# Gate and up matrices loaded as two halves of 64 partitions with 16 KB runs instead of two halves of 128 partitions with 8 KB runs

## The reference, cut to what matters

```python
D_MODEL = 1024; SEQ = 256; DEPTH = 2; N_EXPERTS = 16; D_EXPERT = 512
"moe_w_gate": nrm(ks[21], (DEPTH, N_EXPERTS, D, D_EXPERT), D),
"moe_w_up":   nrm(ks[22], (DEPTH, N_EXPERTS, D, D_EXPERT), D),
"moe_w_down": nrm(ks[23], (DEPTH, N_EXPERTS, D_EXPERT, D), D_EXPERT),

    for e in range(N_EXPERTS):
        hdn = jax.nn.silu(xt @ w_gate[e]) * (xt @ w_up[e])
        y = y + combine[:, e:e + 1] * (hdn @ w_down[e]).astype(jnp.float32)
```

## Time and profile before

| | us |
|---|---|
| time before, median of 3 runs | 886.97 (886.14 to 888.75) |
| the profiled execution | 886.78 |
| its span | 885.0 |
| busy in the span: PE | 842.0 |
| DVE | 329.7 |
| ACT | 177.5 |
| POOL | 159.8 |

### The profile page before, as it was taken

One profiled execution on the slowest core, in us unless ns is written; L12 is line 12 of the kernel. 1 busy time (PEld: TensorE's weight loads), 2 busy tenths in 40 slices (PEclk: granted clock), 3 DMA queues, 4 the chain that ended last, 5 costly groups with the idle time before them and its releaser, 6 DMA issues.

```text
span 885.0 us, 11785 instructions
## 1 busy us (share of the span) xinstructions
PE 842.0 (95%) x4341; PEld 465.4 (53%) x4341; DVE 329.7 (37%) x598; ACT 177.5 (20%) x356; POOL 159.8 (18%) x269
## 2 busy tenths in 40 slices
PE   5999999999999899999999869999899999999996
PEld 3788444444444455455545337774545555545552
DVE  2835766856302322111112058777511112211114
ACT  2100112112102221222121132240322122112112
POOL 0023000000003531122210122300632212012111
PEclk9999999999999999999999899999899999999999
DMA  9989999998569599999999996679889999989994
GB/s 317 387 308 375 375 363 337 339 380 346 230 244 372 206 405 422 421 420 422 422 422 420 371 403 264 238 292 423 324 331 421 422 421 420 384 317 422 421 404 129
DMA packets 70014, 317.29 MB, mean 359 GB/s; under 512 B 10039, under 2 KB 10170, under 8 KB 44366
## 3 DMA queue, kind: packets, MB, share of 16 engines
q1 hardware_dynamic: 61594, 304.42, 85.7%
q0 software_dynamic: 4976, 8.40, 3.1%
q10 hardware_dynamic: 3396, 3.80, 1.4%
HBM read 311.31 MB, written 15.20 MB: 369 GB/s over the span
## 4 chain that ended last, share of the span: by engine, by line
PE 81%; DMA 8%; SPq 5%; DVE 3%; issue 2%; ACT 1%; ACTq 0%; POOL 0%; DVEq 0%; POOLq 0%
PE bank L730 12%; PE bank L912 12%; PE bank L930 11%; PE bank L899 10%; PE bank L771 6%; PE bank L874 6%; PE bank L671 5%; SPq L470 4%; PE bank L1129 3%; DMA acc<-in_moe_w_up 3%; DMA ring<-in_w_mod 2%; PE bank L723 2%; DMA part<-outs 1%; PE bank L1083 1%; PE bank L922 1%
## 5 line engine op out<-in xcount | busy, mean ns | idle before, releaser
L1793 DVE TENSOR_TENSOR arena<-bank,arena 128x256 f32<-128x256 f32 x34 | 21.0, 617 | 254.4 <-PE bank L912 254.4
L1542 DVE SCALAR_TENSOR_TENSOR part<-ring,cpad,part 128x1024 f32<-128x1024 f32 x84 | 111.1, 1323 | 4.1 <-DMA ring<-in_w_mod 1.2
L730 PE MATMUL bank<-ring,xnT 128*128 128x512 f32 x256 | 111.2, 592 | 0.0
L899 PE MATMUL bank<-ring,arena 128*64 128x512 f32 x416 | 92.1, 595 | 0.0
L930 PE MATMUL bank<-ring,arena 128*64 128x512 f32 x352 | 81.7, 606 | 4.3 <-issue 4.3
L912 PE MATMUL bank<-ring,arena 128*64 128x256 f32 x704 | 80.3, 381 | 0.2 <-issue 0.2
L730 PEld LDWEIGHTS bank<-ring,xnT 128*128 128x128 f32 x256 | 48.4, 190 | 59.4 <-issue 59.3
L874 PEld LDWEIGHTS bank<-arena,y 128*128 128x128 f32 x544 | 64.6, 198 | 15.4 <-issue 15.4
L874 PE MATMUL bank<-arena,y 128*128 128x128 f32 x544 | 67.5, 284 | 1.4 <-DVE arena L1753 1.4
L912 PEld LDWEIGHTS bank<-ring,arena 128*64 128x64 f32 x704 | 50.2, 137 | 30.2 <-issue 8.6
L1317 ACT ACTIVATE arena<-bank,modc,scale 128x128 f32<-128x128 f32 x68 | 25.6, 457 | 182.5 <-PE bank L874 182.5
(11 more groups left out here) (342 smaller groups left out, 1066.9 us busy)
## 6 DMA issues: line engine op xcount, KB each, us to landing
ring<-in_w_mod SPq DMA_DIRECT2D x48, 1024.0 KB, 12.3
ring<-in_moe_w_gate SPq DMA_DIRECT2D x48, 1024.0 KB, 15.5
ring<-in_moe_w_down SPq DMA_DIRECT2D x44, 1024.0 KB, 12.7
ring<-in_moe_w_up SPq DMA_DIRECT2D x40, 1024.0 KB, 12.7
ring<-in_ret_w_in SPq DMA_DIRECT2D x24, 1024.0 KB, 7.4
arena<-in_moe_w_down SPq DMA_DIRECT2D x12, 1024.0 KB, 17.0
arena<-in_moe_w_up SPq DMA_DIRECT2D x12, 1024.0 KB, 16.6
arena<-in_moe_w_gate SPq DMA_DIRECT2D x9, 1024.0 KB, 10.5
```

The lines of the kernel that those rows point to most:

```text
L730: ins = pe.matmul(pair[tt][:], xnT[:, k, tok(tt)], w[:, k, :], start=(k == 0), stop=(k == KT - 1))
L899: ins = pe.matmul(bank[0][e * 64:(e + 1) * 64, :], xgT[:, k, e * 64:(e + 1) * 64], w(e, k), start=(k == 0), stop=(k == KT - 1))
L1542: ins = dve.scalar_tensor_tensor(o, w[:, k, :], c, o, ALU.mult, ALU.add)
```

## The change

For a gate or up matrix whose buffer is undivided, a transfer now carries all 16 KB of 64 partitions (0 to 63, then 64 to 127), where it carried 8 KB of all 128. The bytes, the number of transfers and their order are the same. Since each transfer now brings all rows for half of the partitions, a product needs both: `landed_in` waits for both at each call, and SyncE, before it refills a buffer, waits for the event of the second half in both cases when either of the two matrices is loaded in this way. Down matrices, and gate and up matrices in divided buffers, are loaded as before.

```diff
+        def in_one_piece(l, m):
+            return m % 6 < 4 and HOMES[l][m][0] <= RING
...
                 def fill(m, f):
                     w = matrix(l, m // 6, m % 6)
-                    w = w[:, 4 * f:4 * f + 4, :] if m % 6 < 4 else w[:, f]
                     b = HOMES[l][m][0]
-                    sp.dma_start(home(l, m, f), w).then_inc(landed[f][b] if b < RING else outside_in[f][b - RING], 16)
+                    if in_one_piece(l, m):
+                        ps = slice(f * P // 2, (f + 1) * P // 2)
+                        dst = (ring[:, b, :] if b < RING else arena[:, spare:spare + 4096]).rearrange("p (k n) -> p k n", k=KT)[ps]
+                        w = w[ps]
+                    else:
+                        dst = home(l, m, f)
+                        w = w[:, 4 * f:4 * f + 4, :] if m % 6 < 4 else w[:, f]
+                    sp.dma_start(dst, w).then_inc(landed[f][b] if b < RING else outside_in[f][b - RING], 16)
...
-                        used(m - n, f, begun)
+                        used(m - n, 1 if in_one_piece(l, m) or in_one_piece(l, m + 1) else f, begun)
...
                 def landed_in(m, f):
                     b, n = HOMES[l][m]
-                    pe.wait_ge(landed[f][b] if b < RING else outside_in[f][b - RING], 16 * n)
+                    for g in range(2) if in_one_piece(l, m) else (f,):
+                        pe.wait_ge(landed[g][b] if b < RING else outside_in[g][b - RING], 16 * n)
```

## The result

The changed kernel takes 1227.36 us (1218.08 to 1229.53, four runs) where the kernel before took 887.15 beside it: a ratio of 1.382, with a 95% interval of 1.3779 to 1.3861. The prediction was 1070, with a range of 884 to 1100. The direction was right, the size was not: 340 us more, where 183 had been forecast.

A forecast was written before the change was run, and what follows sets the result against it. The DMA queue was taken to bound layer 0's experts and nearly layer 1's. Layer 0 +78 and layer 1 +97 made 175, plus 8 for less lead: +183, so 886.8 becomes 1070 us, range 884 to 1100.

The forecast's parts named there:

- What bounds the kernel: Expert rounds: the DMA queue needs 29.9 us a pair against TensorE's 25.94, setting layer 0's end; layer 1 just favours TensorE.
- The price of a transfer: Each 64-partition transfer of 16 KB runs, bounded from 0.05 us gained to 2.49 us more; 2.25 us more taken.
- the high end of the bounds: Transfers to half the partitions fill half the lanes: 210 GB/s, 4.98 us each, 2.49 more.
- 1.9: Cost factor taken for each new transfer, 2.25 us more, since engines somewhat out of step can fill other lanes part-time.
- Layer 0: Layer 0's experts: 34 loop transfers at 2.25 give 76.5 us, plus 2 for those ahead: +78.
- The idle 28.6 us: Queue idle time between 223 and 305, said to take up the 27 us more of 12 transfers ahead of layer 0's experts.
- Layer 1: Layer 1's experts: 56 transfers cost 126 us more, less idle time and lead: +97; 8 more for less lead on entering and leaving.
- The late refills: Layer 1: SyncE waits for the gate product's end, 3.5 us later, seven times; 0 to 3 us if the queue keeps pace.
- The attention only moves: Attention between the layers: it is only shifted in time, with nothing added.
- an unchanged pace: Rival 1, expert loads: nothing happens to the pace; layer 0 gains 1.7 us, total 885 to 888; chance 0.23.
- the partial case: Rival 2, expert loads: factor 1.6 from long runs, or engines drifting; 1.49 us a transfer, +105, 992; chance 0.13.
- worse than half: Rival 3, expert loads: 4.98 us a transfer plus other queue traffic, 1095, more if halves collide; beyond 1100 chance 0.07.

The follow-up runs named there:

- kept in groups: SyncE waits in the loop for each four transfers to land before issuing more: on the changed kernel 1250.0 us, on the kernel before 1007.7 us.
- every second partition: The change with even partitions, then odd ones, instead of 0 to 63 and 64 to 127, same waits: 892.4 us, single run.
- the run with both waits alone: The kernel before's loads with the change's waits in TensorE and SyncE: 894.03 us over four runs, ratio 1.0079.

## Why the prediction went wrong

*What bounds the kernel* held. The queue sets layer 0's end and nearly sets layer 1's, and a transfer's price came through in full: kept in groups, 90 us for the 85 that fell on layer 0's path. What it left out is the small transfers of another queue, which share the DMA engines with the weights (see the attention below).

*The price of a transfer*: the high end of the bounds, twice the time, is what the runs show (1.259 against 0.611 us for 16 KB). I took 1.9, on the ground that engines somewhat out of step can fill the other lanes. This step failed, and not by its size only but by its sign. Left to run on they lose more than half pace, not less: 142 us in layer 0's loop against 85 at half pace, so 4.2 us a transfer instead of my 2.25. It was my bound that failed too. I let it hold for the new transfers and kept the old pace for the 42 others beside them, though nothing in the trace showed that those would keep it. Had I carried "half" over to the whole queue, the loop would have been 76 x 2.49 = 189 us longer at most, and the measured 142 lies inside (as a mean: single stretches of 6 us of that queue moved only 144 GB/s).

*Layer 0*: +78 forecast, +157.6 measured. Of it 85 is half pace, 57 mostly the loss of the full transfers beside (their packets alone give 54 for the whole layer), and 15 the matrices ahead of the experts, for which I had left 2. The idle 28.6 us of the earlier trace rows were used, all but 7 of them: in the changed kernel the DMA share in those windows is 0.83, 0.90, 0.98 and 1.02. But 12 x 2.49 = 30 us were to go into them and 22 did. The rest, and what the full transfers behind lost, showed as a first round of 32.1 us instead of 27.4.

*Layer 1*: +97 and 8 forecast, +138.1 measured. 56 x 2.49 less the 29 us that were to hide is 110; the remaining 28 are for the most part again the transfers beside, whose 8 KB packets took 23 us of 16 engines more than at 0.317. The late refills, for which I gave 0 to 3 us, cost 6 by themselves; whether any of that is in the 28 is not shown.

*The attention only moves*: this step failed too, by 45.0 us. I counted the queue's bytes and not who else uses it. The 4 KB that another queue brings sits on layer 1's way in, and the row that would have warned was within reach: before, these vectors too landed only as the weight queue ran dry, some 13 us after their issue, in time by luck: the queue had a gap there.

*The rivals*: the one on the other side, an unchanged pace, is what every second partition gives, so such a transfer exists and only its address was wrong. Long runs, which I priced by the instruction fetches' 1.0 us, cost nothing: 0.611 us. That row was of no use for it; why those packets took 1.0 us is not shown. The 1.9, and the partial case but for that row, rested on nothing but the hope of engines filling each other's lanes. The last rival, worse than half, had a chance of 0.07, and it is what came; its 1095 took up neither of the two mechanisms that were missing.

## What to carry to other kernels

Halving a transfer by partitions 0 to 63 and 64 to 127 halves its pace here, whatever the length of the runs; split it along the free dimension or into even and odd partitions instead. When some transfers of a full queue become slower, price those queued beside them too, and the small ones on other queues for which a stage waits: here these two made up some 130 of 342 us. Longer runs, with half as many transfers, gave 0.24%, and only where no refill had to wait longer for them.

## What the runs showed of the hardware

Three things I had not expected. 64 partitions taken in steps of two move at the full 424 GB/s, where 64 in a row move at 215. Transfers over 128 partitions lose pace beside the slow ones: 95% of the 8 KB packets took up to 0.782 us instead of 0.321. And TensorE's granted clock fell with the waits, to 0.75 to 0.81 in the rounds that the queue sets, where it was 1.00 in full ones; its matmuls then took longer (842.0 us busy before, 898.8 after), which cost little since the queue was the one waited for. Where the path goes through TensorE it does cost: 3 us at the end of the run with both waits alone, for eight matmuls behind 3 us of idleness.
